# Two-layer mixer plus a diffusion-style block on one core: weight loads move two blocks ahead of the modulation loads, and ScalarE waits for the loads of x directly

## What is computed

```python
for l in range(2):                                   # first block
    h = rmsnorm(x, g_pre_mix[l])
    parts = split_cols(h @ w_in[l])                  # attention, pooling, SGU, conv inputs; 4 gates
    merged = sum(sigmoid(gate_i) * (branch_i @ w_br_i))
    x = x + rmsnorm(merged @ w_out[l], g_post_mix[l])
    h = rmsnorm(x, g_pre_ffn[l])
    f = (silu(h @ w_ffn_gate[l]) * (h @ w_ffn_up[l])) @ w_ffn_down[l]
    x = x + rmsnorm(f, g_post_ffn[l])

mod   = silu(c) @ w_mod + b_mod                      # second block: 6 * 1024 modulation values
mod_c = silu(c_ctx) @ w_mod + b_mod                  # and those of the context
h  = rmsnorm_2(x, norm1_g) * (1 + sc1) + sh1
hc = rmsnorm_2(ctx, norm1_g) * (1 + sc1c) + sh1c     # 256 context tokens
... neighbourhood attention and gated linear attention on h and hc, merge, SwiGLU
```

## Time and profile before

| | us |
|---|---|
| median of 3 runs | 2541.19 |
| range of the runs | 2539.64 to 2541.27 |
| the profiled execution | 2542.04 |
| its span, first to last instruction | 2540.2 |
| PE busy in it | 2503.8 (99%) |
| POOL busy | 1787.6 (70%) |
| DVE busy | 1134.2 (45%) |
| ACT busy | 585.2 (23%) |
| mean granted TensorE clock | 0.991 |

### The profile page before, as it was taken

The page is one execution under the profiler, slowest core; times in us unless marked ns, Lnnn a source line. Parts: engine busy times, 40 slices in busy tenths (PEclk is TensorE's granted clock), DMA queues, the critical chain, the costliest instruction groups (busy, mean ns, idle before and its releaser), DMA issues.

```text
span 2540.2 us, 33818 instructions
## 1 busy us (share of the span) xinstructions
PE 2503.8 (99%) x11952; PEld 2030.7 (80%) x11952; DVE 1134.2 (45%) x1660; ACT 585.2 (23%) x1006; POOL 1787.6 (70%) x816
## 2 busy tenths in 40 slices
PE   8999999999999999999999999999999999899999
PEld 6877788788878787788878888878888788688887
DVE  6764423644454766442354445566128722311100
ACT  3133311311100313322221111132324520211100
POOL 6766778688888576677868888836353467588887
PEclk9999999999999899999999999999999999999999
DMA  4222222222355222222323235511122223223233
GB/s 142 91 82 75 91 91 91 75 96 94 115 198 190 70 91 83 83 83 91 95 104 99 92 106 190 192 50 59 50 67 84 75 79 95 71 95 99 94 117 104
DMA packets 70208, 250.84 MB, mean 99 GB/s; under 512 B 8304, under 2 KB 8432, under 8 KB 70000
## 3 DMA queue, kind: packets, MB, share of 16 engines
q1 hardware_dynamic: 66528, 239.69, 29.5%
q10 hardware_dynamic: 3600, 9.99, 1.1%
HBM read 247.56 MB, written 2.10 MB: 98 GB/s over the span
## 4 chain that ended last, share of the span: by engine, by line
PE 91%; issue 4%; DVE 2%; POOL 2%; DMA 1%; ACT 0%; POOLq 0%; SPq 0%; DVEq 0%; ACTq 0%
PE bank L487 23%; PE bank L483 23%; PE bank L484 22%; PE bank L429 4%; PE bank L431 4%; PE bank L430 4%; PE bank L795 1%; PE bank L1144 1%; POOL w_hi L398 1%; PE bank L820 1%; PE bank L804 1%; PE bank L1128 1%; POOL w_lo L401 1%; PE bank L1118 1%; DMA w_raw<-weights 0%
## 5 line engine op out<-in xcount | busy, mean ns | idle before, releaser
L398 POOL TENSOR_TENSOR w_hi<-w_raw,one 128x1024 fp32r<-128x1024 f32 x405 | 780.5, 1927 | 711.9 <-PE bank L487 439.8
L401 POOL TENSOR_TENSOR w_lo<-w_raw,w_hi 128x1024 fp32r<-128x1024 f32 x405 | 1008.7, 2491 | 31.9
L483 PE MATMUL bank<-act_hi,w_hi 128*128 128x512 f32 x1808 | 714.8, 395 | 2.9 <-POOL w_hi L398 2.7
L484 PE MATMUL bank<-act_lo,w_hi 128*128 128x512 f32 x1808 | 705.6, 390 | 0.0
L487 PE MATMUL bank<-act_hi,w_lo 128*128 128x512 f32 x1872 | 464.3, 389 | 0.0
L487 PEld LDWEIGHTS bank<-act_hi,w_lo 128*128 128x128 f32 x1872 | 350.9, 188 | 73.4 <-issue 1.0
L483 PEld LDWEIGHTS bank<-act_hi,w_hi 128*128 128x128 f32 x1808 | 340.7, 188 | 81.2 <-issue 9.4
L484 PEld LDWEIGHTS bank<-act_lo,w_hi 128*128 128x128 f32 x1808 | 340.7, 188 | 73.5 <-issue 3.8
L483 PE MATMUL bank<-f_hi,w_hi 128*128 128x512 f32 x528 | 207.2, 392 | 3.2 <-POOL w_hi L398 3.2
L484 PE MATMUL bank<-f_lo,w_hi 128*128 128x512 f32 x528 | 205.6, 389 | 0.0
L487 PE MATMUL bank<-f_hi,w_lo 128*128 128x512 f32 x528 | 131.8, 390 | 0.0
(11 more groups left out here) (447 smaller groups left out, 3528.4 us busy)
## 6 DMA issues: line engine op xcount, KB each, us to landing
w_raw<-weights SPq DMA_DIRECT2D x405, 512.0 KB, 3.4
mod_raw<-mods SPq DMA_DIRECT2D x48, 512.0 KB, 4.6
bias<-bias ACTq DMA_DIRECT2D x8, 512.0 KB, 4.3
resid<-x SPq DMA_DIRECT2D x8, 256.0 KB, 5.3
out<-resid ACTq DMA_DIRECT2D x8, 256.0 KB, 4.3
params<-params ACTq DMA_DIRECT2D x2, 534.5 KB, 4.1
ctx_raw<-ctx ACTq DMA_DIRECT2D x1, 1024.0 KB, 4.8
second<-second ACTq DMA_DIRECT2D x1, 972.5 KB, 7.0
```

The source lines that it names most:

```text
L398: nc.gpsimd.tensor_tensor(w_hi[:, j, :], w_raw[:, j, :], one[:, 0:1].to_broadcast([P, 1024]), ALU.mult)\
L401: nc.gpsimd.tensor_tensor(w_lo[:, j, :], w_raw[:, j, :], w_hi[:, j, :].bitcast(F32), ALU.subtract).then_inc(blocks_split, 1)
L483: mm(out, w_hi[:, slot, tile * P:tile * P + P], rows_hi, start=start, stop=False)
L484: mm(out, w_hi[:, slot, tile * P:tile * P + P], rows_lo, start=False, stop=False)
```

## The change

Two edits. SP loads weight blocks 0 and 1 ahead of its loops, and each load within the loops is that of the block two further on, so that `mods[n]` now stands behind `load(118 + n)` of its layer in place of `load(116 + n)`. The loop after the modulation stage starts one pair later. And ScalarE, in the start, waits for the DMA of x tile k itself and no longer for VectorE's `x_ready`.

```diff
             for k in range(KT):
                 sp.dma_start(resid[:, k, :], io["x"][k]).then_inc(x_loaded[k], 16)
+            for b in range(2):
+                load(b, b)
             with sp.Fori(0, DEPTH) as l:
                 with sp.Fori(0, B_DOWN // 2) as i:
                     for j in range(2):
-                        load(BL * l + 2 * i + j, j)
+                        load(BL * l + 2 * i + j + 2, j)
                 with sp.Fori(0, (BL - B_DOWN) // 4) as i:
                     for j in range(4):
-                        load(BL * l + B_DOWN + 4 * i + j, j % 2)
+                        load(BL * l + B_DOWN + 4 * i + j + 2, j % 2)
                         n = 24 * l + 4 * i + j
                         sp.wait_ge(mod_used, n + 3)
                         sp.dma_start(mod_raw[:, j % 2, :], mods[n]).then_inc(mod_loaded[j], 16)
 
             sp.dma_start(swap, io["swap"]).then_inc(swap_loaded, 16)
-            with sp.Fori(B2 // 2, NB // 2) as i:
+            with sp.Fori(B2 // 2 + 1, NB // 2) as i:
...
             act.wait_ge(g_pre_loaded, 16)
             for k in range(KT):
-                act.wait_ge(x_ready, k + 1)
+                act.wait_ge(x_loaded[k], 16)
```

## The result

The changed kernel takes 2543.61 us in the median of 20 runs (2537.07 to 2549.88), the kernel before 2539.89 in 20 runs beside it (2530.45 to 2545.3). The ratio is 1.0023, 95% interval 1.0013 to 1.0032: 3.7 us slower. The forecast was 2540.6 and 0.6 faster. The time lies in the range that was given, the direction does not.

A forecast was written before the change was run, and what follows sets the result against it. PE, busy 99% of the span, was taken as the bound. Terms -3.7 - 2.1 + 0.2 - 1.1 + 5.1 + 1.0 = -0.6 us, set on the median 2541.2, gave 2540.6; range 2535.3 to 2545.3.

The forecast's parts named there:

- start, ScalarE's edit: First 25 us: ScalarE squares tile 6 earlier, so block 0 ends earlier; gain 3.8 read, 3.7 us taken.
- down stage, layer 0: Layer 0's down stage: earlier weight loads remove PE's 2.13 us wait on GpSimd's split; gain 2.1 us.
- end of layer 0: Layer 0's end: the last modulation block comes later and PE waits for mod_used; cost 0.2 us, between 0 and 1.8.
- down stage, layer 1: Layer 1's down stage: the same kind of wait on GpSimd's split goes; gain 1.1 us.
- end of layer 1: Layer 1's end: late block 22 pushes context_low into GpSimd's splits, so PE waits for the spread tile; cost 5.1 us.
- more time at 1.2 GHz: After PE's wait at layer 1's end: possible lower clock, mostly hidden by the sums; cost 1.0 us, between -1 and +5.
- the laying: Layer 1's end: context_low's 8 operations placed into GpSimd's timetable, from 1655.5 to 1665.05 us.
- Rival B: PE's gap at layer 1's end: late modulation block starves VectorE, clock falls; some 2553 or 2546.7 us; chance 0.10.
- Rival C: Start: ScalarE's edit gains nothing, limited by PE's sums or lost again at a later VectorE wait; 2544.3 us; chance 0.10.
- part 1: Start: ScalarE waits for the x tile loads themselves and no longer for VectorE; gain taken as 3.7 us.
- A: Layer 1's end: the delay does not reach PE, as blocks land early enough or VectorE finds gaps; 2534.5 us; chance 0.15.
- D: Weights' queue: worth more than PE's two waits, half of the 7.0 us left also going; 2537 us; chance 0.05.

The follow-up runs named there:

- e5: The changed kernel with VectorE's context work moved ahead of the late modulation blocks at layer 1's end; 2536.69 us against 2537.52, ratio 0.9993.
- e7: The changed kernel with context_low reading one operand from PSUM instead of SBUF (wrong data, same operation count and size); 2535.38 us, ratio 0.9985.
- e2: The kernel before with only the weights' load order changed, ScalarE waiting as before; 2545.37 us, ratio 1.0027.
- e3: The changed kernel, both edits kept, with weights loaded one block ahead in place of two; 2535.51 us, ratio 0.9991.
- e6: The changed kernel with 20 spare matmuls on PE in its wait for the spread tile at layer 1's end; 2543.92 us, ratio 1.0018.
- e11: Second set of the kernel before with only the weights' load order changed; 2544.22 us, ratio 1.0018.
- e12: The kernel before with 10 or 20 extra VectorE operations at the head of layer 1's context_low; 2545.36 us (1.0035) and 2547.21 us (1.0043).
- e8: The changed kernel with weights one block ahead and VectorE's context work ahead of the late modulation blocks; 2539.0 us, ratio 0.9993.
- e10_before_again: The kernel before, unchanged, run again as a kernel of its own; 2538.63 us, ratio 1.0.

## Why the prediction was wrong

The kernel was taken apart at the starts of GpSimd's splits, and in each part but the first half of the time at 1.2 GHz was taken off. The first row is as measured, since its forecast holds 1.2 us of clock too. The profiles fall into groups by what the part contains (the old order is that of the weights before, a lead is one or two blocks ahead); means of each, in us:

| term | forecast | measured | from |
|---|---|---|---|
| start, ScalarE's edit | -3.7 | -1.6 | end of block 0, 8 profiles without the edit (mean 22.46), 8 with it (20.84); at equal clock 21.8 and 20.8, so -1.0 |
| down stage, layer 0 | -2.1 | -1.6 | blocks 116 to 139: 117.3 in 7 profiles of the old order, 115.7 in 9 with a lead |
| end of layer 0 | +0.2 | +0.4 | blocks 139 to 144: 45.4 in those 7, 45.8 in 7 with a lead of two |
| down stage, layer 1 | -1.1 | -0.8 | blocks 144 to 281: 791.9 and 791.1 in the same |
| end of layer 1 | +5.1 | +4.5 | blocks 281 to 284: 51.3 in 5 profiles, 46.8 in 5 of the old order |
| sum of these | -1.6 | +0.9 | with the start at equal clock +1.5; the fit gives +0.9 (+-0.4) |
| more time at 1.2 GHz | +1.0 | +3.8 | the remainder: 4.7 (means of 32 and 35 runs, +-1.1) less 0.9 |

The row on the end of layer 1 is some 0.5 too small and the clock's as much too large: part of the low clock falls into PE's wait itself (3.1 us in after), where it costs nothing, and was halved away all the same. The first four rows with the start at equal clock give -3.0, and e5 and e7, which keep both edits without the wait, measure -3.35 and -3.4.

**Right: the places and the kind of each cost.** The late modulation blocks, the operations held against GpSimd's splits and the wait of about 5 us for the spread tile came (e2, e3, e7), and so did the end of layer 0, where two of the seven profiles with a lead of two blocks show no wait for `mod_used` and five show 1.0 to 1.5.

**Right in part by luck: 5.1 at the end of layer 1.** Put into the times of the kernel before (8.8 later), block 22 landed at 1653.6, where 1653.9 was forecast. But it was used up only at 1657.1 in place of 1655.5, since VectorE was not free to take it: its queue had been late since block 20, and the operations for the context behind that block were held as well. The prediction had followed block 22 alone. Against this, `context_low` then took 8.4 us where the laying gave 9.55, with three operations held long, fewer than the four of the kernel before. 1.6 too little and 1.1 too much left an error of 0.6.

**Wrong, first: "I take 1.0" for the clock in the wait.** The price was set as if the sums' own wait for VectorE hid most of it; some 3.3 to 3.8 were measured, inside its bounds of -1 to +5 but far from the value taken. Kernels in which PE waits about 5 us for the spread tile, or is filled there (after, e2, e6, e11, e12), have mean clocks of 0.9889 to 0.9898, over 86 runs 0.9893; the others have 0.9898 to 0.9914, over 218 runs 0.9910. The two lowest of the others are e5 and e8, so the wait is not the only thing that lowers it. e12_wait10 shows that this wait by itself, in the kernel before, brings it: a mean clock of 0.9893, and 8.1 us for a wait of 4.9. Rival B named the place and had 5 us or more for it, at 0.10; its second mishap, a landing of 6.2 us, was not needed. Its picture, low clock in the wait's wake, is only part of it, though: e6_filled keeps PE busy there and still pays, with the low clock in the third window. Why a late spread tile brings more of the lower clock than the idle time itself explains stays open.

**Wrong, second: "Gain 3.8" at the start and "Gain 2.1" in layer 0.** Both were read off one execution as if each ran so. It had the late course of the start, in which VectorE's two `raw_lo` collide with GpSimd's first split. Of the 8 profiles without ScalarE's edit, 4 ended block 0 late (23.3 to 24.9) and 4 early (20.3 to 20.7); with the edit all 8 lie at 20.3 to 21.4. The edit takes away the late course, whose price was read rightly (3.5 us between the profiles of before and after, for 3.8), and gives next to nothing in the early one. The wait of 2.13 us in the down stage belonged to the same execution: in 6 others of the old order it was 0.95 to 1.33.

What would have turned the sum is the two together: 2.6 us of gain too much and 2.8 of clock too little, from -0.6 to +4.7 in the means (+3.7 in the medians). Rival C, that part 1 does nothing, was half right and for another reason; A and D are out: the wait reached PE, and nothing came beyond the waits that were seen.

No version here beats the kernel before by much. The best is ScalarE's edit alone, 0.9982 (0.9969 to 0.9994). e5_ctx_first keeps both edits without the price and is 3.35 better at equal clock, yet in the runs only 0.9993 (0.9979 to 1.0007).

## What to carry to other kernels

When a load is moved back in a queue, follow it, and each load ahead of it that moved too, to whatever stands behind their user, and lay those operations into the other engine's timetable; that part of the working came out within 0.6 us, though of two errors that nearly cancel, and the one came of following the last load alone. A term read off one profile is one draw: where an order between two engines is decided by a margin of a microsecond (a square starting at 9.4 to 9.8 or at 10.4 to 10.7, against a split at 11.5), take the mean of both courses, not the one that the profile happens to show. And a wait put into the bottleneck engine can be dearer than its length: here 4.9 us cost about 8 (5.3 to 12.4).

## What the runs showed of the hardware

**The same kernel, two paces at the start.** Whether the start takes the early or the late course goes with the pace of TensorE's first sums: VectorE's square of tile 5, ahead of the `raw_lo` pair, waits for a sum, 1.24 us in the earlier trace rows. Windows of PE, in the profile of before and in that of e10_before_again:

```profile
9.00:11.00 2.00, 2.00 (x4) 1.00 1.05 408
```

```profile
9.00:11.00 2.00, 2.00 (x6) 1.00 1.06 412
```

Both read a granted clock of 1.00, but one does four matmuls of the sums in these 2 us and the other six: they take 0.86 us each up to some moment and 0.43 after it. In the 16 profiles that moment lies between about 8 and 11 us. PEclk does not show this; the counts do.

**A long low stretch in code that was not changed.** Windows of PE in after, e10_before_again (the kernel before) and before:

```profile
1916.00:1932.00 16.00, 16.00 (x111) 0.59 0.26 82
```

```profile
1916.00:1932.00 16.00, 16.00 (x95) 0.77 0.37 132
```

```profile
1916.00:1932.00 16.00, 16.00 (x151) 1.00 0.37 125
```

PE is busy throughout in all three. Of the 16 profiles 8 have a stretch of 13.7 us at 1.2 GHz there, with or without the edits; the part from block 300 to 340 then takes 331.5 to 332.0 us and otherwise 325.5 to 325.7. That is 6 us, more than the change itself, and one reason why single executions of one kernel lie 15 us apart while the medians of before repeat within 3. What brings it is not shown.
